# One core, two transformer blocks: each expert's result returned to the tokens by itself, in two rounded parts, with a plain one-hot matrix

## The reference, cut to what matters

```python
def swiglu(h, w1, w3, w2):                       # w1, w3: 1024 x 2816, w2: 2816 x 1024
    return (silu(h @ w1) * (h @ w3)) @ w2

def moe_swiglu(h, router_w, w1, w3, w2):         # 8 experts, top 2 of 8 per token
    t = h.reshape(256, 1024)
    top_vals, top_idx = lax.top_k(t @ router_w, 2)
    top_w = softmax(top_vals)
    gates = sum(one_hot(top_idx, 8) * top_w[..., None], axis=1)   # 256 x 8, two entries per row
    out = zeros_like(t)
    for e in range(8):
        out = out + gates[:, e:e + 1] * swiglu(t, w1[e], w3[e], w2[e])
    return out
```

## Time and profile before

| | |
|---|---|
| three runs | 2931.55, 2932.46, 2935.47 us; median 2932.46 |
| span of the profiled execution | 2930.2 us; no time of its own is listed beside it |
| TensorE busy, VectorE, ScalarE, GpSimd | 2883.4, 2031.7, 1626.6, 300.7 us |
| mean granted TensorE clock | 0.996 of 2.4 GHz |
| HBM read | 608.99 MB, 208 GB/s over the span |
| experts' stage | about 861 to 1645 us of the span |

### The profile page before, as it was taken

The page is one execution under the profiler, slowest core; times in us unless marked ns, Lnnn a source line. Parts: engine busy times, 40 slices in busy tenths (PEclk is TensorE's granted clock), DMA queues, the critical chain, the costliest instruction groups (busy, mean ns, idle before and its releaser), DMA issues.

```text
span 2930.2 us, 46621 instructions
## 1 busy us (share of the span) xinstructions
PE 2883.4 (98%) x20144; PEld 2666.9 (91%) x20144; DVE 2031.7 (69%) x1842; ACT 1626.6 (56%) x1603; POOL 300.7 (10%) x224
## 2 busy tenths in 40 slices
PE   8999999999999999999999999999999999999999
PEld 8999999999988888888888696999899999896999
DVE  6787665678768888888888775654665565575653
ACT  6456544545657767767767562544754454362542
POOL 1130210113010000000000002210011011002110
PEclk9999999999999999999999999999999999999999
DMA  7444555544449989889989640556365646540553
GB/s 237 159 140 155 183 180 180 187 145 144 159 173 370 350 343 375 348 339 353 377 333 373 204 154 15 180 177 210 111 187 176 198 145 186 189 144 30 158 184 119
DMA packets 359731, 613.26 MB, mean 209 GB/s; under 512 B 11520, under 2 KB 323926, under 8 KB 324577
## 3 DMA queue, kind: packets, MB, share of 16 engines
q1 hardware_dynamic: 355936, 597.99, 58.5%
q10 hardware_dynamic: 3104, 12.10, 1.2%
q0 software_dynamic: 480, 0.12, 0.0%
HBM read 608.99 MB, written 1.05 MB: 208 GB/s over the span
## 4 chain that ended last, share of the span: by engine, by line
PE 96%; DVE 1%; ACT 1%; DMA 0%; issue 0%; POOL 0%; ACTq 0%; SPq 0%; DVEq 0%; POOLq 0%
PE ps L329 19%; PE ps L331 19%; PE ps L330 19%; PE ps L1272 5%; PE ps L1274 5%; PE ps L1273 5%; PE ps L1248 3%; PE ps L1250 3%; PE ps L1249 3%; PE ps L1813 2%; PE ps L689 2%; PE ps L1828 2%; PE ps L1322 1%; PE ps L1781 1%; PE ps L1769 1%; PE ps L1291 1%
## 5 line engine op out<-in xcount | busy, mean ns | idle before, releaser
L273 DVE TENSOR_TENSOR wlo<-raw,whi 128x2048 fp32r<-128x2048 f32 (+2 forms) x574 | 1317.0, 2300 | 451.8 <-ACT whi L262 432.6
L262 ACT ACTIVATE whi<-raw 128x2048 fp32r<-128x2048 f32 (+2 forms) x574 | 1084.4, 1891 | 259.9 <-PE ps L331 136.3
L329 PE MATMUL ps<-HX,whi 128*128 128x256 f32 x1808 | 521.4, 288 | 16.3 <-DVE wlo L273 11.6
L331 PE MATMUL ps<-HX,wlo 128*128 128x256 f32 x1808 | 512.5, 283 | 0.0
L330 PE MATMUL ps<-HX,whi 128*128 128x256 f32 x1808 | 512.4, 283 | 0.0
L329 PE MATMUL ps<-HXB,whi 128*128 128x256 f32 x1760 | 501.3, 285 | 2.7 <-DVE HXB L448 2.7
L330 PE MATMUL ps<-HXB,whi 128*128 128x256 f32 x1760 | 498.6, 283 | 0.0
L331 PE MATMUL ps<-HXB,wlo 128*128 128x256 f32 x1760 | 498.6, 283 | 0.0
L329 PEld LDWEIGHTS ps<-HX,whi 128*128 128x128 f32 x1808 | 347.8, 192 | 22.6 <-ACT HX L524 10.3
L330 PEld LDWEIGHTS ps<-HX,whi 128*128 128x128 f32 x1808 | 347.9, 192 | 3.4 <-issue 3.3
L331 PEld LDWEIGHTS ps<-HX,wlo 128*128 128x128 f32 x1808 | 347.7, 192 | 0.0
(11 more groups left out here) (337 smaller groups left out, 4228.8 us busy)
## 6 DMA issues: line engine op xcount, KB each, us to landing
raw<-in_c_experts SPq DMA_DIRECT2D x264, 1024.0 KB, 4.9
raw<-in_w_in SPq DMA_DIRECT2D x71, 1024.0 KB, 5.0
raw<-in_ff_w_gate SPq DMA_DIRECT2D x44, 1024.0 KB, 5.3
raw<-in_ff_w_up SPq DMA_DIRECT2D x44, 1024.0 KB, 5.3
raw<-in_ff_w_down SPq DMA_DIRECT2D x32, 1024.0 KB, 5.2
raw<-in_dense_w SPq DMA_DIRECT2D x30, 1024.0 KB, 5.3
raw<-in_hy_w_in SPq DMA_DIRECT2D x24, 1024.0 KB, 5.3
raw<-in_ff_w_down SPq DMA_DIRECT2D x16, 768.0 KB, 4.7
```

The costliest lines, as they stand in the source:

```text
L262: e.activation(m.whi[:, i % NSPLIT, 0:n], m.raw[:, i % NRAW, 0:n], ACT.Copy).then_inc(*k.up("act", "hi", i))
L273: e.tensor_tensor(m.wlo[:, i % NRAW, 0:n], m.raw[:, i % NRAW, 0:n], hi, ALU.subtract).then_inc(*k.up("dve", "lo", i))
L329: e.matmul(o, wh, xh, start=first and t == k0, stop=False)
L331: i = e.matmul(o, wl, xh, start=False, stop=final and t == k1 - 1)
```

## The change

The expert's result is multiplied by its gate on the way out of PSUM and split into a high and a low part: ScalarE writes the high part (`YR` part 0) with the slot's gate as its scale, VectorE the low part (`YR` part 1). The slots' gates are the row sums of the transposed `SG`: ScalarE reads that bank twice with an accumulator (into a scratch tile, `once more`), and VectorE compares the same bank with zero, which gives a plain one-hot slot x token, `SELT`. Both are float32r, so the return is made of float32r matmuls: per expert 8 chunks x 2 parts, 256 columns. It stands after block j = 1 of every next expert, and once after the last. VectorE's comparison stands after block j = 2 of a pair's second expert, behind ScalarE's gather copies; its two low parts stand at the end of each expert.

```diff
--- before.py
+++ after.py
@@ -158,6 +158,8 @@
         self.HT = [rounded("HTH", 0, [128, 22, 128]), rounded("HTL", 1.5, [128, 22, 128])]
         self.GT = [rounded("GT0", 3, [128, 8, 2, L]), rounded("GT1", 5, [128, 8, 2, L])]
         self.SELR = rounded("SELR", 8, [128, 2, 2, 128])
+        self.SELT = rounded("SELT", 8.25, [128, 2, 2, L])
+        self.YR = rounded("YR", 10, [128, 2, D])
         self.HXB = rounded("HXB", 6, [128, 2, T8, L])
         self.rs = sb("rs", [128, L])
         self.rst = self.lbt[:, 32:34]
@@ -1175,8 +1177,8 @@
     v["across"] = m.buf(9)[0:8, 0:L]
     v["iota"], v["upper"] = m.buf(9)[:, 1024:1152], m.buf(9)[:, 1152:1280]
     v["SG"] = m.buf(8)[:, 1536:2048].rearrange("p (j e n) -> p j e n", j=2, e=2)
-    v["SGT"] = [m.buf(8)[:, 512 + 512 * i:1024 + 512 * i].rearrange("p (e n) -> p e n", e=2) for i in range(2)]
-    v["Y"] = m.buf(10).rearrange("p (e n) -> p e n", e=2)
+    v["once more"] = m.buf(9)[:, 1536:2048].rearrange("p (e n) -> p e n", e=2)
+    v["slot gates"] = m.small[:, 196:200].rearrange("p (q e) -> p q e", q=2)
     v["sil"] = m.buf(11)[:, 0:1024].rearrange("p (a n) -> p a n", a=2)
     v["hf"] = m.buf(11)[:, 1024:2048].rearrange("p (a n) -> p a n", a=2)
     v["TX"] = [m.HX[:, p].rearrange("p t n -> p (t n)").rearrange("p (j n) -> p j n", j=2) for p in range(2)]
@@ -1228,8 +1230,8 @@
                 pe_expert_block(e, k, m, o, G, i, j, "ab", s, x, j, w)
             if j >= 1:
                 pe_turn_hidden(e, k, m, v, s, x, j - 1)
-            if j == 1 and i == 0 and p > 0:
-                pe_scatter(e, k, m, v, s, p - 1)
+            if j == 1 and x > 0:
+                pe_scatter(e, k, m, v, s, x - 1)
             if j == 2 and i == 1 and p < 3:
                 pe_gather(e, k, m, v, s, p + 1)
         if i == 1:
@@ -1255,7 +1257,7 @@
             k.note("mm", "used", n)
             if j == 0:
                 pe_turn_hidden(e, k, m, v, s, x, 5)
-    pe_scatter(e, k, m, v, s, 3)
+    pe_scatter(e, k, m, v, s, 7)
     return flag
 
 
@@ -1311,17 +1313,18 @@
     mm.then_inc(*k.up("mm", "sgt", s, p))
 
 
-def pe_scatter(e, k, m, v, s, p):
+def pe_scatter(e, k, m, v, s, x):
+    p, i = divmod(x, 2)
     e.wait_ge(*k.at("free", "sgt", s, p))
     for c2 in range(4):
-        e.wait_ge(*k.at("y", s, 2 * p + 1, c2 // 2))
-        o = pe_take(e, k, m, "back", s, p, c2)
+        e.wait_ge(*k.at("y", s, x, c2 // 2))
+        o = pe_take(e, k, m, "back", s, x, c2)
         for c in range(2):
             ch = 2 * c2 + c
-            for i in range(2):
-                mm = e.matmul(o[:, c * L:(c + 1) * L], v["Y"][:, i, ch * 128:ch * 128 + 128], v["SGT"][p % 2][:, i, :],
-                              start=i == 0, stop=i == 1)
-        mm.then_inc(*k.up("mm", "back", s, p, c2))
+            for part in range(2):
+                mm = e.matmul(o[:, c * L:(c + 1) * L], m.YR[:, part, ch * 128:ch * 128 + 128], m.SELT[:, p % 2, i, :],
+                              start=part == 0, stop=part == 1)
+        mm.then_inc(*k.up("mm", "back", s, x, c2))
 
 
 def act_router_in(e, k, m, a):
@@ -1375,13 +1378,12 @@
         if x == 7:
             e.wait_ge(*k.at("gt free", s, 2))
             act_hyena_loads(e, k, m, a, 0)
-        if i == 0 and p > 0:
-            e.wait_ge(*k.at("back", s, p - 1, 3))
+        if x:
+            e.wait_ge(*k.at("back", s, x - 1, 3))
         for c in range(2):
             e.wait_ge(*k.at("ey", s, x, c))
-            e.activation(v["Y"][:, i, c * 512:c * 512 + 512], ps(k, m, "ey", s, x, c)[:, :], ACT.Copy).then_inc(
-                *k.up("act", "free", "ey", s, x, c))
-            k.note("act", "y", s, x, c)
+            e.activation(m.YR[:, 0, c * 512:c * 512 + 512], ps(k, m, "ey", s, x, c)[:, :], ACT.Copy,
+                         scale=v["slot gates"][:, p % 2, i:i + 1]).then_inc(*k.up("act", "yh", s, x, c))
     return flag
 
 
@@ -1405,9 +1407,10 @@
     k.note("act", "gt", s, p)
     e.wait_ge(*k.at("sgt", s, p))
     if p >= 2:
-        e.wait_ge(*k.at("back", s, p - 2, 3))
-    e.activation(v["SGT"][p % 2], ps(k, m, "sgt", s, p)[:, :].rearrange("p (e n) -> p e n", e=2), ACT.Copy).then_inc(
-        *k.up("act", "free", "sgt", s, p))
+        e.wait_ge(*k.at("y", s, 2 * p - 3, 1))
+    for i in range(2):
+        e.activation(v["once more"][:, i, :], ps(k, m, "sgt", s, p)[:, i * L:i * L + L], ACT.Copy,
+                     accum_out=v["slot gates"][:, p % 2, i:i + 1]).then_inc(*k.up("act", "slot gates", s, p))
 
 
 def dve_moe(e, k, m, panels, s, last):
@@ -1479,6 +1482,7 @@
     e.tensor_tensor(v["gates"], v["oh1"], v["oh2"], ALU.add).then_inc(*k.up("dve"))
     dve_gated(e, k, m, v, s, 0)
     flag = crowded_flag(e, k, m)
+    dve_turned_places(e, k, m, s, 0)
     for x in range(8):
         p, i = divmod(x, 2)
         for j in range(6):
@@ -1496,8 +1500,10 @@
             k.note("dve", "hf", s, x, j)
             if j >= 1:
                 dve_turn_hidden(e, k, m, s, x, j - 1)
-            if j == 1 and i == 0 and p > 0:
-                dve_scatter(e, k, m, s, p - 1)
+            if j == 1 and x > 0:
+                dve_scatter(e, k, m, s, x - 1)
+            if j == 2 and i == 1 and p < 3:
+                dve_turned_places(e, k, m, s, p + 1)
             if j == 1 and i == 1 and p < 3:
                 dve_places(e, k, m, v, s, p + 1)
                 dve_gated(e, k, m, v, s, p + 1)
@@ -1505,7 +1511,13 @@
             dve_panel(e, k, m, panels)
             if j == 0:
                 dve_turn_hidden(e, k, m, s, x, 5)
-    dve_scatter(e, k, m, s, 3)
+        for c in range(2):
+            e.wait_ge(*k.at("yh", s, x, c))
+            cs = slice(c * 512, c * 512 + 512)
+            e.scalar_tensor_tensor(m.YR[:, 1, cs], ps(k, m, "ey", s, x, c)[:, :], v["slot gates"][:, p % 2, i:i + 1],
+                                   m.YR[:, 0, cs].bitcast(F32), ALU.mult, ALU.subtract).then_inc(*k.up("dve", "free", "ey", s, x, c))
+            k.note("dve", "y", s, x, c)
+    dve_scatter(e, k, m, s, 7)
     return flag
 
 
@@ -1540,12 +1552,21 @@
             e.tensor_scalar(v["SG"][:, j, i, :], v["iota"], rc, ge, ALU.is_equal, ALU.mult).then_inc(*k.up("dve", "gated", s, p))
 
 
-def dve_scatter(e, k, m, s, p):
+def dve_turned_places(e, k, m, s, p):
+
+    e.wait_ge(*k.at("slot gates", s, p))
+    if p >= 2:
+        e.wait_ge(*k.at("back", s, 2 * p - 3, 3))
+    src = ps(k, m, "sgt", s, p)[:, :].rearrange("p (e n) -> p e n", e=2)
+    e.tensor_scalar(m.SELT[:, p % 2], src, 0.0, None, ALU.is_gt).then_inc(*k.up("dve", "free", "sgt", s, p))
+
+
+def dve_scatter(e, k, m, s, x):
     for c2 in range(4):
-        x = m.X[:, 2 * c2:2 * c2 + 2, :]
-        e.wait_ge(*k.at("back", s, p, c2))
-        e.tensor_tensor(x, x, ps(k, m, "back", s, p, c2)[:, :].rearrange("p (a n) -> p a n", a=2), ALU.add).then_inc(
-            *k.up("dve", "free", "back", s, p, c2))
+        to = m.X[:, 2 * c2:2 * c2 + 2, :]
+        e.wait_ge(*k.at("back", s, x, c2))
+        e.tensor_tensor(to, to, ps(k, m, "back", s, x, c2)[:, :].rearrange("p (a n) -> p a n", a=2), ALU.add).then_inc(
+            *k.up("dve", "free", "back", s, x, c2))
 
 
 def pool_numbers(e, k, m, s, last):
```

## The result

The changed kernel takes 2927.46 us (median of 19 runs, 2924.71 to 2929.33), the one before 2933.25 (19 runs, 2930.76 to 2935.52): 5.8 us less, ratio 0.9981, 95% interval 0.9975 to 0.9988. Two more sets of 11 runs of the same kernel gave 0.9980 (0.9971 to 0.9990) and 0.9986 (0.9976 to 0.9995). The forecast was 2926.9.

What follows compares the result with a forecast made beforehand. TensorE's own instructions were taken to bound the experts' stage. -20.5 + 13.2 + 1.4 + 0.1 + 0.2 = -5.6 us, from 2932.5 to 2926.9 us; range 2922.5 to 2931.5.

Steps and rivals of the forecast that it cites:

- The price of a return: TensorE inside the experts' loop: three pair returns at 6.83 us go, seven single-expert returns at 1.88 come, net 7.3 us less.
- The bounds around the 7.3: Net saving on TensorE's stream: 6.9 us at 0.129 us a matmul, 8.6 at 0.107.
- VectorE's added work: Experts' stage: additions, low parts and comparisons add 23 us on VectorE, which has 109 us idle there.
- the tight place: Start of experts 1, 3, 5, VectorE without a gap: gather's seventh tile waits 0.45 us more, three times, 1.35 us back.
- Rival 3: Whole experts' stage: VectorE takes over, its added work finds no cover, 14.3 us slower, about 2946.8 us; chance 5%.
- rival 4: Returns on TensorE: rounded matmuls go at the full-precision pace, 27.3 us more, about 2959.8 us; chance 2%.
- The lead I had found for the twelfth panel: Start of experts 1, 3, 5: VectorE's first subtraction ends 0.8 us before TensorE's panel instead of 1.24, no stall.
- Loop gained: Experts' loop: 7.3 us saved on TensorE less 1.4 us of added waits, 5.9 us gained.
- rival 2: Bigger stalls at experts 1, 3, 5 (3 us, not 1.4) and 1.5 us for a poorer clock: 2930 us; chance 13%.
- The end: After the last panel: the shorter return gains nothing because a 7.85 us branch in TensorE's queue holds the sums, 0.1 later.
- Rival 1: End of stage: the branch's end follows TensorE's last matmul, so 2.4 us more are gained, 2924.5 us; chance 20%.
- The clock: Around the branch at the stage's end: longer TensorE idling lowers the granted clock, 0.2 us more (1.4 less to 1.9 more).

## Why the prediction was right

**The price of a return** was read off rows of the same kinds and held: 6.83 us forecast for a pair's (an expert with one takes 99.59 us, without 92.69: 6.90), 1.88 for an expert's (94.59: 1.90). Net 7.3 forecast, 3 x 6.90 - 7 x 1.90 = 7.4 measured. The bounds around the 7.3 were added up wrong: with the terms as they stand, 0.129 a matmul gives 6.6 and not 6.9, and 0.107 gives 9.1 and not 8.6. The range would be 0.5 us wider at its lower end and 0.3 at its upper; nothing else hangs on it.

**VectorE's added work**, 23 us forecast and 21 measured, was hidden but for the tight place: no wait of TensorE stands at the experts' ends inside the loop, at the even experts or behind the comparison. Rival 3 fell with that, rival 4 with the 1.99 us of a return.

**The tight place** was named with its bank and its line, and is the term that was mis-sized: 0.45 us a gather forecast, 1.35 in all; beyond a matmul's pace the three new gaps came to 1.9 and 1.8 us in two traces and, with the twelfth panel, to 3.7 in the first. The difference of 2.4 against 1.96 us was right, and where VectorE entered its chain on time the wait was as forecast, 0.47 (experts 1 and 3, two traces). But I took VectorE to enter its chain as early as before everywhere. It enters as early as its last high part lets it. In experts 1 and 3 of the second and third traces its product starts 11.91 us before the gather's first matmul; in expert 5 it starts 11.55, 11.48 and 11.57 us before it in the three traces, after a high part had waited 0.56, 0.82 and 0.56 us for its weights, and the gather's wait is 0.83, 0.91 and 0.82. The lead I had found for the twelfth panel, 0.8 us, held in expert 3 (0.76) and was used up in expert 1 in one trace. Loop gained: 5.9 forecast, 3.6, 5.5 and 5.6 measured. That is rival 2's mechanism, at a third of its extra price in two traces and over all of it in one.

**The end** held: branch forecast 4.0 us after the last panel, 3.7 measured; sums 11.9, measured 11.91 to 11.95. Rival 1 (2.4 us gained there) is excluded, most plainly by the third trace of the changed kernel. There the return ran at a granted clock of 1.00; its last addition ended 6.2 us after the last panel, 2.3 sooner than before, as forecast, and TensorE's last matmul of the return started 4.9 us after it instead of 5.9 and 6.3. The sums started at 11.91 all the same. Timeline of that trace, changed kernel:

```profile
1634.74 2.15 PE L1325 MATMUL ps<-SELT,YR 128*128 128x256 f32 x16 [2.85 <-DVE YR L1517]
1635.49 2.48 DVE L1568 TENSOR_TENSOR X<-X,ps 128x512 f32<-128x512 f32 x4 [0.19 <-PE ps L1325]
1638.07 2.19 ACT L365 ACTIVATE work<-X 128x512 f32<-128x512 f32 x4 [5.18 <-DVE X L1568]
...
1643.61 5.19 PEld L358 LDWEIGHTS ps<-work,ones 128*128 128x128 f32 x16 [6.92 <-issue]
```

The two kernels without the branch show 1.65 us of what lay hidden behind it. That is less than the 2.2 forecast, because the rounded return ran at the lower clock in that trace (granted 0.50 from 1636 to 1638 us): 3.1 us from its first matmul to its last instead of 1.9. The Trainium skill's rule of the fetch behind a taken branch (page "Runtime: NRT & Kernel Launch", section "Instruction fetch mechanics") agrees with what moved: in the three kernels in which the branch starts 1.5 to 2.6 us sooner than in the kernel they are compared with, it ends 1.0 to 2.4 us sooner, and it lasts 8.28 to 8.52 us. No trace shows what the 8 us consist of, nor that they are a fetch.

**The clock** was 0.2 us forecast. Windows view of 18 us from the last panel, before and changed (second trace), columns as in the earlier trace rows:

```profile
1637.00:1655.00 18.00, 13.46 (x52) 10.76 (x52) 5.04 (x5) 5.29 (x10) 0.00 (x0) 0.91 0.94 296
```

```profile
1632.00:1650.00 18.00, 9.96 (x35) 8.38 (x35) 6.26 (x7) 4.94 (x8) 0.00 (x0) 0.62 0.95 295
```

A mean of 0.62 instead of 0.91 (0.72 in the first trace and 0.81 in the third): with 3 and 6 us of idle time around the return, the lower level covers 7 to 14 of the 18 us, where before it covered some 3.4. It costs little, because TensorE mostly waits there: from the sums to the filters 5.4 to 6.1 us in the three traces instead of 5.2, so 0.2 to 0.8.

So -5.6 came out as -5.8, -5.2 and -4.6 in three sets: the stream and the end right, the tight place 0.4 to 2.3 us too cheap. That the first set lies within 0.2 us of the forecast is partly luck: up to the filters (loop and end together) the three traces show 2.7, 5.1 and 5.3 us gained, and the one with the least belongs to the set with the most. The forecast of 2926.9 also started from the median of three runs, 2932.46, where 19 runs gave 2933.25; its time is 0.6 us under the measured one.

## What to carry to other kernels

Price a change of matmul type by rows of the same kind and shape in the same trace, and count what stands behind it: a panel's first step took 0.42 us behind a full-precision return, 0.31 behind a transpose and 0.23 behind a rounded return. When work is added to an engine with slack, look for the stretch in which it has none and follow every bank and buffer that this stretch frees; moving VectorE's one-hots to an expert with slack won another 4.5 and 1.8 us on top of the 5 of the change. Where a view says "issue", look for the instruction in the queue: a branch that starts once the last wait before it is over can hide everything that happens to finish while it lasts.

## What the runs showed of the hardware that was not expected

The taken branch in TensorE's queue lasts 7.85 to 8.71 us in ten traces, on ScalarE and VectorE 54 and 72 ns; without it the next block's filters start 4.0 us (before) to 6.0 us (changed, second trace) sooner after the last panel. And while the loads keep the DMA engines 94% busy (changed kernel, experts' stage), a single panel can be waited for 2.2 us: of three traces of the same kernel one shows it, in front of VectorE's tight stretch.
